# Two transformer blocks on one core: bulk transfers cut and moved, context keys in plain order, a finer end

## The reference

```python
def first_block(x, c, ctx, c_ctx, ...):
    # layer 0: q, k, v, o, z, gates, pool inputs = xm @ w_in for context and latent tokens
    hc_f, st_f = mlstm_scan(qc, kc, vc, lic[0], lfc[0], zero)      # state of the context
    hl_f, _ = mlstm_scan(ql, kl, vl, lil[0], lfl[0], st_f)         # and both backwards
    y_l = even_out(hl_f + flip(hl_b), ol, zml, upl, zpl, ...)      # norm, gates, pooling
    x = layer_norm(ALPHA * x + g_l * (y_l @ w_out_even), g0, b0)
    # layer 1
    y_l = sgu_mixer(xm_l, w_in_odd, sgu_ln_g, sgu_ln_b, w_sp, b_sp)
    return layer_norm(ALPHA * x + g_l * (y_l @ w_out_odd), g1, b1)

def second_block(x, mem, positions, ...):
    hn = rmsnorm(h, norm_mix_w)                                    # "the second norm"
    h = h + merged(retention(hn), rg_lru(hn)) @ w_mix_out
    h = h + memory_cross_attention(rmsnorm(h), rmsnorm(mem), w_q, w_k, w_v, w_o)
    h = h + conv_gated_ffn(rmsnorm(h), w_up, conv_w, conv_b, w_down)
    return rmsnorm(h, final_norm_w)
```

## Time and profile before

| | us |
|---|---|
| median of 3 runs | 3110.17 (3110.03 to 3110.28) |
| the profiled execution | 3113.6 |
| its span, first to last instruction | 3111.8 |
| TensorE busy | 3043.6 |
| VectorE busy | 2143.5 |
| ScalarE busy | 1582.1 |
| GpSimd busy | 49.6 |

### The profile page before, as it was taken

The page is one execution under the profiler, slowest core; times in us unless marked ns, Lnnn a source line. Parts: engine busy times, 40 slices in busy tenths (PEclk is TensorE's granted clock), DMA queues, the critical chain, the costliest instruction groups (busy, mean ns, idle before and its releaser), DMA issues.

```text
span 3111.8 us, 44843 instructions
## 1 busy us (share of the span) xinstructions
PE 3043.6 (98%) x16776; PEld 2605.8 (84%) x16776; DVE 2143.5 (69%) x2709; ACT 1582.1 (51%) x1945; POOL 49.6 (2%) x52
## 2 busy tenths in 40 slices
PE   7899999999999999999999999999999999999998
PEld 5678878888888887888888888888888888888887
DVE  3378878788587787647668865567567777777544
ACT  3355444556644566544566654445445555555443
POOL 0031100000000000000000000000000000000000
PEclk9999999999999999999999999999999999999999
DMA  9966857886578655655555555565455555555554
GB/s 391 369 220 237 293 186 287 301 314 213 190 254 293 237 188 191 202 170 190 185 183 168 183 189 190 180 231 193 141 163 188 189 187 187 188 188 190 189 188 141
DMA packets 180247, 666.41 MB, mean 214 GB/s; under 512 B 20084, under 2 KB 20468, under 8 KB 178808
## 3 DMA queue, kind: packets, MB, share of 16 engines
q1 hardware_dynamic: 178424, 660.09, 61.8%
q10 hardware_dynamic: 1664, 4.19, 0.3%
HBM read 657.91 MB, written 6.29 MB: 213 GB/s over the span
## 4 chain that ended last, share of the span: by engine, by line
PE 85%; DVE 6%; DMA 4%; ACT 2%; DVEq 1%; issue 1%; SPq 0%; ACTq 0%
PE acc L765 46%; PE acc L769 23%; PE acc L776 3%; PE acc L778 3%; PE acc L777 3%; DVE w_lo L2015 2%; DMA ada_more<-in_w_ada 1%; DMA mod_raw<-in_w_mod 1%; ACT w_hi L1288 1%; DMA raw<-in_w_mix_out 1%; PE acc L944 1%; DVE mod_raw L2026 0%; DMA raw<-in_w_xa_k 0%; PE msc L813 0%; PE msc L890 0%
## 5 line engine op out<-in xcount | busy, mean ns | idle before, releaser
L2015 DVE TENSOR_TENSOR w_lo<-raw,w_hi 128x1024 fp32r<-128x1024 f32 x1020 | 1240.8, 1226 | 619.4 <-ACT w_hi L1288 609.1
L1288 ACT CAST w_hi<-raw 128x1024 fp32r<-128x1024 f32 x1020 | 1061.7, 1048 | 846.4 <-PE acc L769 585.7
L765 PE MATMUL acc<-a_pair,w_hi 128*128 128x512 f32 x2944 | 933.7, 399 | 10.8 <-DVE w_lo L2015 8.2
L769 PEld LDWEIGHTS acc<-a_pair,w_lo 128*128 128x128 f32 x2944 | 555.4, 189 | 131.5
L765 PE MATMUL acc<-b_pair,w_hi 128*128 128x512 f32 x1792 | 570.7, 400 | 16.4 <-DVE w_lo L2015 16.4
L769 PE MATMUL acc<-a_pair,w_lo 128*128 128x256 f32 x2944 | 580.4, 279 | 0.0
L765 PEld LDWEIGHTS acc<-a_pair,w_hi 128*128 128x128 f32 x2944 | 452.4, 190 | 13.7 <-issue 4.7
L765 PE MATMUL acc<-f_pair,w_hi 128*128 128x512 f32 x1408 | 442.4, 395 | 0.0
L769 PEld LDWEIGHTS acc<-b_pair,w_lo 128*128 128x128 f32 x1792 | 337.6, 188 | 80.0
L769 PE MATMUL acc<-b_pair,w_lo 128*128 128x256 f32 x1792 | 353.0, 278 | 0.0
L769 PEld LDWEIGHTS acc<-f_pair,w_lo 128*128 128x128 f32 x1408 | 264.5, 188 | 62.5
(11 more groups left out here) (359 smaller groups left out, 2467.1 us busy)
## 6 DMA issues: line engine op xcount, KB each, us to landing
raw<-in_w_ffn_up SPq DMA_DIRECT2D x176, 512.0 KB, 3.9
mod_raw<-in_w_mod SPq DMA_DIRECT2D x128, 512.0 KB, 5.3
raw<-in_w_ffn_down SPq DMA_DIRECT2D x88, 512.0 KB, 3.3
ada_more<-in_w_ada SPq DMA_DIRECT2D x40, 512.0 KB, 14.6
raw<-in_w_xa_k SPq DMA_DIRECT2D x32, 512.0 KB, 12.7
raw<-in_w_k SPq DMA_DIRECT2D x32, 512.0 KB, 4.3
raw<-in_w_v SPq DMA_DIRECT2D x32, 512.0 KB, 5.2
raw<-in_w_even_out SPq DMA_DIRECT2D x32, 512.0 KB, 4.7
```

Of the source, the lines that this page charges most:

```text
L765: pe.matmul(acc[:, bank(stage, g) + m, :], w_h[:, cols], pair[:, :, kc, :], start=begin, stop=False, skip_group_check=True)
L769: mm = pe.matmul(acc[:, bank(stage, g) + m, 0:T], w_l[:, cols], pair[:, 0, kc, :], start=False, stop=end, skip_group_check=True)
L1288: nc.scalar.copy(w_hi[:, slot], source).then_inc(hi_done, 1)
L2015: vec.tensor_tensor(w_lo[:, slot], source, w_hi[:, slot].bitcast(F32), ALU.subtract).then_inc(lo_done, 1)
```

## The change

- ctx_k is no longer woven: group 0 (units 0 to 3), the gates' two units, then groups 1 to 3.
- `mask` is loaded beside lat_v's unit 10, `pool_mat` and `ang_i` beside lat_q's units 1 and 3, `pool_w` in two halves beside lat_o's units 7 and 11, after a wait for the end of the mLSTM. The attention's keys and values go in four halves of 1024 KB beside mix_out's units 10, 14, 18 and 22.
- Modulation sums: lat_q has 9 for 11, lat_o 12 for 13, pool_u 9 for 10, even_out 12 for 8.
- The first low part of the SGU's operand is made at unit 6 and not 7.
- Column sums and root of the second norm come two units later (17 and 18 for 15 and 16).
- The end: in the last unit TensorE finishes the first bank before the second, each half is copied, added, squared and summed by TensorE by itself, ScalarE loads the table of the root before, and the last multiplications and transfers are eight of two chunks for four of four.

Left out of the diff are new semaphores, counts that waits compare with, and the two calls of `last_group`.

```diff
@@ -117,7 +117,7 @@
-    Stage("ctx_k", "w_k", "F", 1, gate=True, act=1, dve=1, woven=True),
+    Stage("ctx_k", "w_k", "F", 1, gate=True, act=1, dve=1),
...
@@ -192,8 +192,8 @@
-          "lat_q": (0, 1, 2, 4, 5, 6, 8, 9, 10, 12, 13), "lat_o": spread(16, 13), "pool_u": spread(16, 10),
-          "mlstm_z": spread(16, 14), "pool_z": spread(16, 11), "even_out": range(0, 16, 2), "sgu_u": spread(32, 18), "sgu_z": spread(26, 14)}
+          "lat_q": (0, 2, 4, 5, 7, 8, 10, 11, 13), "lat_o": spread(16, 12), "pool_u": spread(16, 9),
+          "mlstm_z": spread(16, 14), "pool_z": spread(16, 11), "even_out": range(0, 24, 2), "sgu_u": spread(32, 18), "sgu_z": spread(26, 14)}
...
@@ -225,10 +225,11 @@
+SGU_LOW_AT = 6
-MIX_SUMS_AT = 15
-MIX_NORM_AT = 16
+MIX_SUMS_AT = 17
+MIX_NORM_AT = 18
...
@@ -648,6 +650,19 @@
+                        if stage.name == "lat_v" and j == 10:
+                            sp.wait_ge(pe_step, AFTER["states"]["pe"])
+                            nc.sync.dma_start(mask[:], t["mask"]).then_inc(mask_in, 16)
+                        if stage.name == "lat_q" and j == 1:
+                            nc.sync.dma_start(pool_mat[:], t["pool_mat"]).then_inc(mask_in, 16)
+                        if stage.name == "lat_q" and j == 3:
+                            nc.sync.dma_start(ang_i[:], t["positions"].partition_broadcast(P)).then_inc(ret_in, 16)
+                        if stage.name == "lat_o" and j in (7, 11):
+                            sp.wait_ge(pe_step, AFTER["mlstm"]["pe"])
+                            half = slice(0, 4) if j == 7 else slice(4, 8)
+                            nc.sync.dma_start(pool_w[:, half, :], t["pool_w"][:, half, :]).then_inc(pool_in, 16)
...
@@ -662,13 +677,14 @@
-                        if stage.name == "mix_out" and j == 10:
+                        if stage.name == "mix_out" and j in (10, 14, 18, 22):
-                            nc.sync.dma_start(flat(xa_kf), t["mem_k"]).then_inc(xa_in, 16)
-                            nc.sync.dma_start(flat(xa_vt), t["mem_v"]).then_inc(xa_in, 16)
+                            kept, stored = (xa_kf, t["mem_k"]) if j < 18 else (xa_vt, t["mem_v"])
+                            half = slice(0, 2 * D // 2) if j % 8 == 2 else slice(2 * D // 2, 2 * D)
+                            nc.sync.dma_start(flat(kept)[:, half], stored[:, half]).then_inc(xa_in, 16)
...
@@ -680,16 +696,6 @@
-                if stage.name == "lat_o":
-                    sp.wait_ge(unit_used, used(STAGE["lat_v"]))
-                    nc.sync.dma_start(mask[:], t["mask"]).then_inc(mask_in, 16)
-                    nc.sync.dma_start(pool_mat[:], t["pool_mat"]).then_inc(mask_in, 16)
-                    nc.sync.dma_start(ang_i[:], t["positions"].partition_broadcast(P)).then_inc(ret_in, 16)
-                if stage.name == "pool_u":
-                    sp.wait_ge(pe_step, AFTER["mlstm"]["pe"])
-                    nc.sync.dma_start(pool_w[:], t["pool_w"]).then_inc(pool_in, 16)
...
@@ -704,10 +710,10 @@
-            for q in range(4):
+            for q in range(8):
-                nc.sync.dma_start(t["out"][:, 4 * q:4 * q + 4, :], y_out[:, 4 * q:4 * q + 4, :]).then_inc(y_stored, 16)
-            sp.wait_ge(y_stored, 4 * 16)
+                nc.sync.dma_start(t["out"][:, 2 * q:2 * q + 2, :], y_out[:, 2 * q:2 * q + 2, :]).then_inc(y_stored, 16)
+            sp.wait_ge(y_stored, 8 * 16)
...
@@ -755,6 +761,17 @@
+                        if stage is LAST and last:
+                            for m in range(2):
+                                for c in range(chunks):
+                                    kc = chunks * k + c
+                                    cols = slice(c * 2 * P + m * P, c * 2 * P + (m + 1) * P)
+                                    pe.matmul(acc[:, bank(stage, g) + m, :], w_h[:, cols], pair[:, :, kc, :], start=False,
+                                              stop=False, skip_group_check=True)
+                                    mm = pe.matmul(acc[:, bank(stage, g) + m, 0:T], w_l[:, cols], pair[:, 0, kc, :], start=False,
+                                                   stop=(c == chunks - 1), skip_group_check=True)
+                                mm.then_inc(unit_used if m else first_bank_used, 1)
+                            continue
...
@@ -1219,10 +1236,12 @@
-            for h in range(8):
-                pe.wait_ge(dve_done, DVE_DONE["ffn_down"] - 2 * (7 - h))
-                mm = pe.matmul(msc[:, 0, 0:T], ones[:], (buf_c if h % 2 else buf_b)[:, h // 2, :], start=(h == 0), stop=(h == 7))
+            pe.wait_ge(dve_done, DVE_DONE["ffn_down"] - 2)
+            pe.matmul(msc[:, 0, 0:T], ones[:], buf_b[:, 0, :], start=True, stop=False)
+            for m in range(2):
+                pe.wait_ge(act_done, ACT_DONE["ffn_down"] - 1 + m)
+                mm = pe.matmul(msc[:, 0, 0:T], ones[:], buf_a[:, 2 + m, :], start=False, stop=(m == 1))
...
@@ -1298,6 +1317,22 @@
+            def last_group(stage, g, n_used):
+                nc.scalar.activation(tiny[:, 0:1], tiny[:, 21:22], ACT.Sqrt)
+                act.wait_ge(acc_free, (stage.iters - 1) * stage.groups + (stage.g0 + g + 2))
+                act.wait_ge(first_bank_used, stage.iters * stage.groups)
+                nc.scalar.copy(halves_b[:, 0:1, :], low_part(stage, g)[:, 0:1, :]).then_inc(half_copied, 1)
+                act.wait_ge(unit_used, n_used)
+                nc.scalar.copy(halves_b[:, 1:2, :], low_part(stage, g)[:, 1:2, :]).then_inc(half_copied, 1)
+                def squares():
+                    for m in range(2):
+                        act.wait_ge(dve_done, DVE_DONE["ffn_down"] - 1 + m)
+                        nc.scalar.activation(buf_a[:, 2 + m, :], x[:, DC - 2 + m, :], ACT.Square).then_inc(act_done, 1)
+                return squares
...
@@ -1953,18 +1990,19 @@
-                    if first < DC - 2:
-                        weighted(first)
+                    ran(weighted(first))
-                ran(mm)
+                return mm
-            rms("final")
-            weighted(DC - 2)
+            steps.wait(pe=1)
+            steps.done(nc.scalar.activation(spare[:], msc[:, 0, 0:T], ACT.Sqrt, bias=tiny[:, 21:22], scale=1.0 / D))
+            steps.done(weighted(DC - 2))
+            steps.end("final")
...
@@ -2060,6 +2098,15 @@
+            def last_group(stage, g):
+                for m in range(2):
+                    dve.drain()
+                    dve.wait_ge(half_copied, 1 + m)
+                    vec.tensor_tensor(buf_a[:, 2 + m, :], main_part(stage, g)[:, m, :], halves_b[:, m, :], ALU.add)
+                    dve.drain()
+                    ran(vec.tensor_tensor(x[:, DC - 2 + m, :], x[:, DC - 2 + m, :], buf_a[:, 2 + m, :], ALU.add))
...
@@ -2137,16 +2186,18 @@
-            def pair_step(hi, lo, make, q, name):
-                if 2 <= q < 10:
-                    p = q - 2
-                    steps.wait(act=p + 1)
-                    vec.tensor_tensor(lo[:, 2 * p:2 * p + 2, :], buf_a[:, 2 * (p % 2):2 * (p % 2) + 2, :],
-                                      hi[:, 2 * p:2 * p + 2, :].bitcast(F32), ALU.subtract).then_inc(pair_ready, 1)
+            def pair_low(hi, lo, p):
+                steps.wait(act=p + 1)
+                vec.tensor_tensor(lo[:, 2 * p:2 * p + 2, :], buf_a[:, 2 * (p % 2):2 * (p % 2) + 2, :],
+                                  hi[:, 2 * p:2 * p + 2, :].bitcast(F32), ALU.subtract).then_inc(pair_ready, 1)
+            def pair_step(hi, lo, make, q, name, first_low_done=False):
+                if 2 + first_low_done <= q < 10:
+                    pair_low(hi, lo, q - 2)
...
@@ -2610,8 +2661,10 @@
+                if j == SGU_LOW_AT:
+                    pair_low(b_hi, b_lo, 0)
-                    pair_step(b_hi, b_lo, lambda q: normalised(2 * q, 2), SGU_NORM_AT[j], "sgu_pair")
+                    pair_step(b_hi, b_lo, lambda q: normalised(2 * q, 2), SGU_NORM_AT[j], "sgu_pair", first_low_done=True)
...
@@ -2972,9 +3025,12 @@
-                    sums = buf_c if g % 2 else buf_b
-                    ran(vec.tensor_tensor(sums[:, first // 4, :], two[:, 0:T], two[:, T:2 * T], ALU.add))
+                    total = vec.tensor_tensor(buf_b[:, min(first, 1), :], two[:, 0:T], two[:, T:2 * T], ALU.add)
+                    if first:
+                        dve.drain()
+                        total = vec.tensor_tensor(buf_b[:, 0, :], buf_b[:, 0, :], buf_b[:, 1, :], ALU.add)
+                    ran(total)
...
@@ -2982,10 +3038,13 @@
-            dve.wait_ge(act_done, ACT_DONE["ffn_down"])
-            for q in range(4):
-                part = y_out[:, 4 * q:4 * q + 4, :]
-                steps.done(vec.tensor_tensor(part, part, bcast(rstd, 4), ALU.mult))
+            for q in range(8):
+                if q == 0:
+                    dve.wait_ge(act_done, ACT_DONE["ffn_down"])
+                if q == 7:
+                    steps.wait(act=2)
+                part = y_out[:, 2 * q:2 * q + 2, :]
```

(12 more changed lines are left out.)

## The result

The changed kernel takes **3086.62 us** (median of 4 runs, 3085.41 to 3086.76), the kernel before 3110.23 beside it (3110.03 to 3110.76). The ratio is 0.9923, with a 95% interval of 0.9906 to 0.9940. That is 23.6 us less where 25.6 was forecast; 3086.62 lies in the range and 2.0 above the predicted time.

What follows compares the result with a forecast made beforehand. TensorE's matmul stream was the bound (busy 3043.6 of 3111.8 us), leaving idle and half-clock time to win. 7.9 + 4.0 + 0.9 - 1.8 + 0.75 + 5.9 + 6.45 + 1.5 = 25.6 off median 3110.17 gives 3084.6; range 3079.0 to 3092.5.

Steps and rivals of the forecast that it cites:

- ctx_k: Context keys, not woven: waits of 2.52 and 3.75 us become one of 1.3; gain 7.9 us (bounds 1.2 and 8.3).
- Rival 1: Context keys: the convolution still covers unit 14, so the stage gains 1.2 instead of 7.9; 3091.3 us, chance 0.10.
- The mLSTM: Before the mLSTM products: earlier transfers and two sums fewer cut 4.98 us idle to 2.4; gain 4.0 (2.5 to 5.1).
- VectorE was late because a modulation chunk landed 3.41 late: Before the mLSTM: a chunk behind three bulk transfers delayed masks and lat_q's last evacuation, leaving TensorE idle 4.98 us.
- even_out: Four more modulation sums at units 16 to 22 load VectorE; waits grow, cost 1.8 us (bounds 0 and 4.9).
- sgu_v: First low part at unit 6; the 6.18 us VectorE-ScalarE loop stays, so 0.75 of 4.0 us remain (bounds 0 and 4.0).
- Second norm, keys and values: Norm two units later gains 5.9 us (4.5 to 6.2); attention's keys and values in four pieces gain 6.45 (4 to 6.45).
- loads are issued 16.0 before TensorE wants them: Mix_out: a reserve of 16 us against at most 4.4 us delay behind a quarter piece, so no stall.
- Rival 4: SyncE's single queue: each of six large bulk pieces stalls the weights behind it, 6.45 us each; 3123.3 us, chance 0.03.
- The end: Chain after the last matmul, worked in half banks: 13.2 us instead of 14.7; gain 1.5 (0.5 to 2.5).
- the gains are differences within one execution, so they go off the median: Final sum: 25.6 us subtracted from the median 3110.17, though the profiled execution was 3.4 over it; gives 3084.6 us.
- the seven idle times of the earlier trace: TensorE's idle stretches where the change works, each read from the timeline; the forecast put them together at 22.3 us.

## Why the prediction was right, and where it was not

**ctx_k.** Right: 8.0 for 7.9, with a wait of 1.22 at unit 3 (1.3) and none at unit 14. Rival 1 is out. Missed: ctx_v is 0.5 longer, with a new wait of 0.27 for the low part of weights at its unit 4 (up to 0.85 in other traces of the changed kernel); the forecast priced only the stage itself.

**The mLSTM.** The size was right (3.8 for 4.0, idle 2.20 for 2.4), its reason was not. The step that failed is "VectorE was late because a modulation chunk landed 3.41 late": that chunk was one of two delays, and each of the two edits alone ends all but 0.7 of what both end, so the gain belongs to neither, and by the runs the move of the transfers is worth nothing beside the fewer sums. The part was costed as one sum and could not tell. That the size was met is in part luck: the clock fell for 3.4 us behind the 2.20 here and not at all in three other traces, and there the gain would have been 1.5 more, over the upper bound of 5.1.

**even_out.** Right: waits at units 21 and 29, of 0.60 and 1.05 (0.25 + 0.4, and 1.4), 1.6 for 1.8.

**sgu_v.** Right in kind: the loop kept its 6.18 and only about 1 us came. What was off is the size of what it holds back. The forecast counted 3.2 for opening it, what is left of the idle time and half clock at 775.33; the run shows 4.0.

**Second norm, keys and values.** 6.1 for 5.9 and 6.5 for 6.45. The step "loads are issued 16.0 before TensorE wants them" was set against a landing, and should have been 13.6; the worst load behind a piece lands 8.5 - 4.0 = 4.5 later than the median (bound: 4.4), so the conclusion holds with less room. Rival 4 is out: no piece, not even of 2 MB, stalls the stream. The rule on transfers of 1 MiB and more (the Trainium skill, "DMA: Bandwidth & Descriptors", "Bandwidth") is not tested by this: the pieces of 1 and of 2 MB (3086.62 and 3086.53) are both at or over its mark. Of the halves of `pool_w`, which are under it, no run tells: the one with `pool_w` in one piece (3086.39) changed other transfers too.

**The end.** 12.9 us after the last product for 13.2. The copy, the two additions and the square of the last half take 1.64 where 2.60 stood (0.96 for 0.9), the eight multiplications 4.91 for 4.96.

**The sum.** The term that failed is the base: "the gains are differences within one execution, so they go off the median". The gains were read from an execution that was longer than is usual, as its 3.4 over the median could have told. By the traces the change brings 27.1, of which 1.0 is mem_k's, an accident of the execution (in the eleven later traces of variants of the changed kernel mem_k ends between 161.8 and 163.8). By the medians it brings 23.6. So the forecast's 25.6 was 1.5 too little for the traces and 2.0 too much for the medians: two errors that work against each other, and that is luck. With 27.1 off the same median it would have said 3083.1, 3.5 below what was measured. Where the 3.5 between them come from stays open. The mean clock of the executions speaks for the clock (the 2.9, 1.5, 2.6 and part of the 4.0 are half clock). The runs point at a second place: undone in the changed kernel, ctx_k costs 7.1 by the medians, the second norm 6.6, and sums and bulk together 3.8, where the two traces have 7.5 (with ctx_v), 6.1 and 3.2, but keys and values in one go only 3.4 where the two traces differ by 6.5. The load behind the 4 MB landed after 15.76 there and after 17.45 and 16.94 in the two traces of before; whether the untraced executions of before also had the shorter landing can't be seen.

One sum of the forecast was added wrongly: the seven idle times of the earlier trace rows make 23.0, not 22.3. Nothing else hangs on it.

## What to carry to other kernels

Before crediting an edit with a stall that two delays share, ask whether either alone would end it: undone one by one, both looked worthless here, and together they are worth 3.8 us. Where VectorE and ScalarE hand work back and forth inside the loop that feeds TensorE, look at the period: if it is constant and above TensorE's (6.18 against 5.44), try putting one side's step a unit later; here it opened the loop at no cost in work. A bulk transfer between streamed loads cost nothing here as long as the worst load behind it landed within the reserve, which is landing time less idle time in a trace that has the stall (13.6 us); cut it only as small as that asks.

## What the runs showed of the hardware

Whether TensorE's clock falls after an idle time is not settled by its length. The same 2.20 us before the mLSTM (2.20 or 2.21 in eight traces) was followed by 3.4 us at half clock in five and by none in three (in the changed kernel it set in at 421.4, 1.1 us after TensorE had begun again); 2.52 us in ctx_k never (three traces); behind 2.50 and 2.47 us at sgu_v's start it fell in both traces of the kernel before, and behind 1.93 in mem_va in the one trace that has it. From the first product of the mLSTM to lat_o 36.1 us passed without the fall, and 37.6 with it: 1.5 us for 3.4 at half clock. The low stretches lasted 3.4 or 6.8 us, and the one in mem_k was of either length in traces of kernels that are the same up to there. So a forecast that counts on the clock should carry some 1.5 to 3.4 us of doubt (an estimate: half of 3.4, as measured, up to half of 6.8) for each such idle time, in each execution anew.
